# Sparse attention's compression in pairs of positions and two steps; all gates of tile 1 of layer 0 beside the first tile's experts

## The reference

```
for each of 2 layers:
  (queries, keys, values, gate logits m_g ...) = split(x @ w_in)
  o_a .. o_d = stick-breaking, sparse (NSA), retention, gated linear attention   # 4 x 256 wide
  proj  = each o @ its w_branch                              # 256 -> 1024
  gates = sigmoid(m_g)                                       # positions x 4 x 1024
  x = layer_norm(al * x + (sum of gates * proj) @ w_out)
  x = layer_norm(al * x + peer_ffn(x))                       # 8 heads x 16 experts per position
```

## Time and profile before

| | us |
|---|---|
| median of 3 runs | 2868.34 |
| lowest, highest | 2865.76, 2875.42 |
| the profiled execution | 2872.7 |
| its span, first to last instruction | 2870.9 |
| PE busy | 2357.6 (82%) |
| DVE busy | 1347.6 (47%) |
| ACT busy | 1304.0 (45%) |
| POOL busy | 749.1 (26%) |
| mean granted TensorE clock, of 2.4 GHz | 0.882 |
| HBM read | 836.06 MB |

### The profile page before, as it was taken

The page is one execution under the profiler, slowest core; times in us unless marked ns, Lnnn a source line. Parts: engine busy times, 40 slices in busy tenths (PEclk is TensorE's granted clock), DMA queues, the critical chain, the costliest instruction groups (busy, mean ns, idle before and its releaser), DMA issues.

```text
span 2870.9 us, 34220 instructions
## 1 busy us (share of the span) xinstructions
PE 2357.6 (82%) x13592; PEld 2004.4 (70%) x13592; DVE 1347.6 (47%) x3159; ACT 1304.0 (45%) x2330; POOL 749.1 (26%) x614
## 2 busy tenths in 40 slices
PE   7989998999999999878676878686788787666676
PEld 6878887877866878767555867566687675565554
DVE  3652333421002323665556764545765544686444
ACT  2741113100000311476746576754567764556665
POOL 0021112200000000333344323333323333434664
PEclk9989999999999999996687998899798999776666
DMA  6221211233435568998799999999998999999997
GB/s 247 105 88 62 85 52 45 81 132 126 162 151 200 197 249 346 402 418 326 283 415 415 411 421 376 392 420 416 391 421 351 420 368 416 404 376 355 421 421 324
DMA packets 110000, 839.35 MB, mean 292 GB/s; under 512 B 12176, under 2 KB 12432, under 8 KB 13968
## 3 DMA queue, kind: packets, MB, share of 16 engines
q0 software_dynamic: 73728, 536.90, 46.3%
q1 hardware_dynamic: 36112, 300.25, 26.6%
HBM read 836.06 MB, written 1.05 MB: 292 GB/s over the span
## 4 chain that ended last, share of the span: by engine, by line
PE 52%; DMA 21%; DVE 11%; ACT 10%; issue 4%; POOL 1%; SPq 0%; POOLq 0%; DVEq 0%; ACTq 0%
DMA mem<-in_puv,mem 20%; PE psm L443 11%; PE psm L2246 7%; PE psm L1816 5%; PE psm L451 5%; DVE mem L2290 4%; PE psm L756 4%; ACT mem L2264 4%; PE psm L2121 3%; PE psm L1351 3%; PE psm L1454 2%; PE psm L2008 2%; ACT L2259 1%; PE psm L1502 1%; PE psm L447 1%
## 5 line engine op out<-in xcount | busy, mean ns | idle before, releaser
L2246 PE MATMUL psm<-mem 128*128 128x128 f32 x4096 | 696.0, 327 | 370.9 <-ACT mem L2264 370.2
L2246 PEld LDWEIGHTS psm<-mem 128*128 128x128 f32 x4096 | 579.2, 170 | 483.7 <-ACT mem L2264 465.2
L2274 POOL DMA_INDIRECT mem<-in_puv,mem x512 | 627.7, 1226 | 1100.4 <-PE psm L2246 1022.4
L2290 DVE CUSTOM_DVE_ANT_0 mem<-mem 128x1024 f32<-128x1024 f32 x512 | 624.8, 1225 | 431.7 <-DMA mem<-in_puv,mem 431.2
L2264 ACT ACTIVATE mem<-mem 128x1024 f32<-128x1024 f32 x512 | 588.8, 1150 | 16.7
L443 PE MATMUL psm<-mem 128*128 128x256 f32 (+2 forms) x1376 | 313.1, 390 | 3.1 <-DVE mem L1291 1.5
L2259 ACT ACTIVATE mem<-mem 128x1 f32<-128x1 f32 x512 | 101.8, 199 | 454.9 <-DVE mem L2290 454.1
L443 PEld LDWEIGHTS psm<-mem 128*128 128x128 f32 x1376 | 261.8, 192 | 53.3 <-issue 14.8
L1816 PE MATMUL psm<-mem 128*128 128x256 f32 x1024 | 245.0, 392 | 0.7 <-ACT mem L1530 0.5
L451 PEld LDWEIGHTS psm<-mem 128*128 128x128 f32 x1440 | 187.0, 195 | 48.8 <-issue 21.9
L451 PE MATMUL psm<-mem 128*128 128x128 f32 x1440 | 199.1, 283 | 23.3 <-DVE mem L1126 6.8
(11 more groups left out here) (364 smaller groups left out, 2414.5 us busy)
## 6 DMA issues: line engine op xcount, KB each, us to landing
mem<-in_w2g SPq DMA_DIRECT2D x64, 1024.0 KB, 8.3
mem<-in_w SPq DMA_DIRECT2D x18, 2048.0 KB, 7.7
mem<-in_pwq SPq DMA_DIRECT2D x32, 1024.0 KB, 11.9
mem<-in_w2f SPq DMA_DIRECT2D x28, 1024.0 KB, 10.5
mem<-in_wgu SPq DMA_DIRECT2D x11, 2048.0 KB, 7.7
mem<-in_w2t SPq DMA_DIRECT2D x20, 1024.0 KB, 11.8
mem<-in_w2b SPq DMA_DIRECT2D x16, 1024.0 KB, 10.6
mem<-in_w2o SPq DMA_DIRECT2D x16, 1024.0 KB, 9.7
```

Source lines behind the costliest of these rows:

```text
L2246: m = pe.matmul(bank(6 + c // 4)[:, tsl(c % 4)], GR[n % PING][:, 1024 + c * 128:1152 + c * 128], ident, is_transpose=True, start=k == 0 an ...
L2274: po.indirect_dma_start(GR[n % PING], None, A[f"puv{i // 2}"], bass.IndirectOffsetOnAxis(ap=IX[i % 2][:, k:k + 1], axis=0)).then_inc(gsem[ ...
L2290: ve.tensor_tensor_reduce(out=GR[n % PING][:, 0:1024], in0=GR[n % PING][:, 0:1024], in1=X[:, i % 2, :], scale=1.0, scalar=0.0, op0=MUL, op ...
```

## The change

The compression takes two positions at a time. `GP_` becomes [key or value][16 pairs][blocks], with the even position's 64 channels in partitions 0 to 63 and the odd one's in 64 to 127; the weights are laid out so outside the kernel. TensorE has 16 matmuls for keys and 16 for values, over 128 partitions, and a `yield` between them puts the two in two plan steps. VectorE writes `GP_` with eight adds instead of two. `nsa` has 23 steps instead of 22, and the streams on ScalarE and VectorE get one empty step more. The exception for tile 1's gates goes: they are woven into its attention in stage 1 as for the other tiles, with banks 0 and 1, and the last 36 steps of tile 0 are mix, query and route alone.

```
--- before.py
+++ after.py
@@ -259,12 +259,11 @@
 
         def tile_steps(i):
             front = ["fm"] * 28 + ["ht1"] * (i == 0) + ["tm"] * 4 + weave([("tm", 10, 1), ("core", 7, 0.7)])
-            attend = weave([("gates", 32 * (i != 1), 1), ("nsa", 22, 1), ("core", 14, 0.7)])
+            attend = weave([("gates", 32, 1), ("nsa", 23, 1), ("core", 14, 0.7)])
             return front + attend + ["mix"] * 24 + ["query"] * 8 + ["route"] * 20
 
         plan = [(s, 0) for s in tile_steps(0)[:-36]]
-        plan += [(s, int(s == "gates")) for s in weave([("mix", 8, 0.5), ("gates", 12, 1)]) + ["query"] * 8
-                 + weave([("route", 20, 1), ("gates", 20, 1)])]
+        plan += [(s, 0) for s in tile_steps(0)[-36:]]
         for i in RI:
             placed_at = [(128.0 * i + k, ("e", 128 * i + k)) for k in range(128)]
             placed_at += [(128.0 * i + 1.1 + 0.1 * k, ("fin", i - 1)) for k in range(4) if i >= 1]
@@ -286,7 +285,7 @@
         used = {}
         uses = dict(fm=[("f", n, 4 * n, min(4 * (n | 1) + 3, 27)) for n in range(7)],
                     tm=[("t", 0, 0, 3)] + [("t", n, 2 * n + 2, (7, 7, 11, 11, 13)[n - 1]) for n in range(1, 6)],
-                    nsa=[("cw", 0, 0, 1)], gates=[("g", n, 2 * n, 4 * (n // 2) + 3) for n in range(16)],
+                    nsa=[("cw", 0, 0, 2)], gates=[("g", n, 2 * n, 4 * (n // 2) + 3) for n in range(16)],
                     mix=[("b", n, 2 * n + 2, 2 * n + 3) for n in R4] + [("o", n, 12 + n, 12 + (n | 1)) for n in R4] + [("ga", 0, 19, 21)],
                     query=[("q", n, 4 * n, 8 * (n // 2) + 7) for n in R8], fin=[("gf", 0, 8, 9)])
         step, nth2, last2 = {}, {}, {}
@@ -1552,8 +1551,6 @@
             if i == 0:
                 pe.wait_ge(*KV[1, 0])
                 pe.wait_ge(*KA[1, 4])
-            if i == 1:
-                pe.wait_ge(*GTA[1, 7])
             pe.matmul(bank(4)[:, 0:128], walpha, LR[0:16, :], start=True, stop=True).then_inc(YP.next((i, "al")), 1)
             yield
             yield
@@ -1798,15 +1795,11 @@
 
 
         def gates_bank(i, j):
-            return bank(4 * (i == 1) + j % 2)
+            return bank(j % 2)
 
         def gates_pe(pe, i):
             t = i % 2
-            if i == 1:
-                pe.wait_ge(*BA_[0, ("m", 0)])
-                pe.wait_ge(*BV[0, ("m", 1)])
-            else:
-                pe.wait_ge(*MA[i, ("t", 5)])
+            pe.wait_ge(*MA[i, ("t", 5)])
             for n in range(16):
                 W = slot2(("g", i, n), 8, 256)
                 pe.wait_ge(*landed2("g", i, n))
@@ -1831,7 +1824,7 @@
 
 
         KS, KW = at(scr, 256), at(scr + 256, 256)
-        GP_ = at(scr + 512, 32, 15)
+        GP_ = at(scr + 512, 2, 16, 15)
         KC, VC = at(scr + 1024, 16), at(scr + 1040, 64)
         PS, PCm, PT = at(scr + 1104, 2, 256), at(scr + 1616, 16), at(scr + 1632, 5, 128)
         NG = SM[:, 24:36]
@@ -1852,14 +1845,15 @@
         def nsa_pe(pe, i):
             t = i % 2
             nb, ns = 7 + 8 * t, 128 * (t + 1)
-            CW = slot2(("cw", i, 0), 32, 64)
+            CW = slot2(("cw", i, 0), 2, 16, 64)
             yield
             pe.wait_ge(*landed2("cw", i, 0))
             pe.wait_ge(*XV[i, "gp"])
-            for k in range(32):
-                pe.matmul(bank(2)[0:64, 0:nb], CW[0:64, k, :], GP_[0:64, k, 0:nb], start=k == 0, stop=k == 31)
-            for k in range(32):
-                m = pe.matmul(bank(3)[0:nb, 64:128], GP_[64:128, k, 0:nb], CW[64:128, k, :], start=k == 0, stop=k == 31)
+            for k in range(16):
+                pe.matmul(bank(2)[0:64, 0:nb], CW[:, 0, k, :], GP_[:, 0, k, 0:nb], start=k == 0, stop=k == 15)
+            yield
+            for k in range(16):
+                m = pe.matmul(bank(3)[0:nb, 64:128], GP_[:, 1, k, 0:nb], CW[:, 1, k, :], start=k == 0, stop=k == 15)
             m.then_inc(XP.next((i, "kc")), 1)
             yield
             for h in R4:
@@ -1920,9 +1915,14 @@
                 for pb in (0, 64):
                     ve.tensor_copy(dst[pb:pb + 64, 0:ns], FK[p0:p0 + 64, 2, 0:ns])
             kv3 = FK[:, 3, :].rearrange("p (c i) -> p i c", i=16)
-            for hf in R2:
-                e = ve.tensor_tensor(GP_[:, 16 * hf:16 * hf + 16, 0:nb], kv3[:, :, hf:hf + nb], bc(posT[:, 16 * hf:16 * hf + 16], 2, nb), ADD)
+            for kv in R2:
+                p = slice(64 * kv, 64 * kv + 64)
+                for par in R2:
+                    for hf in R2:
+                        e = ve.tensor_tensor(GP_[64 * par:64 * par + 64, kv, 8 * hf:8 * hf + 8, 0:nb], kv3[p, par::2, hf:hf + nb],
+                                             bc(posT[p, 16 * hf + par:16 * hf + 16:2], 2, nb), ADD)
             e.then_inc(XV.next((i, "gp")), 1)
+            yield
             yield
             ve.wait_ge(*XP[i, "kc"])
             ve.tensor_copy(KC[0:64, 0:nb], bank(2)[0:64, 0:nb])
@@ -2609,9 +2609,9 @@
         b = I["w_branch_2"][L].reshape(2, 2, 2, 128, 2, 512)
         acc["w2b"].append(b.transpose(4, 0, 3, 1, 2, 5).reshape(4, 128, 2048))
         acc["w2o"].append(chunks(I["w_out_2"][L], 256))
-        ck = [I[n][L].reshape(32, 64, 64).transpose(1, 0, 2).reshape(64, 2048)
+        ck = [I[n][L].reshape(16, 128, 64).transpose(1, 0, 2).reshape(128, 1024)
               for n in ("nsa_cmp_wk_2", "nsa_cmp_wv_2")]
-        acc["cmpw"].append(cat(ck, 0))
+        acc["cmpw"].append(cat(ck, 1))
         wa = np.zeros((128, 128), w.dtype)
         wa[0:16] = I["gla_w_alpha_2"][L]
         pos = I["nsa_cmp_pos_2"][L].T
```

## The result

| | before | after |
|---|---|---|
| median (runs), us | 2871.73 (4) | 2819.95 (4) |
| ratio to the kernel before | | 0.9822, 95% interval 0.9801 to 0.9843 |
| profiled execution, its span, us | 2872.7, 2870.9 | 2820.1, 2818.2 |

The change takes 51 us off by the ratio (51.8 between the medians, 52.7 between the spans). Cut at the same events, the two profiled executions differ so; the last column is what the prediction's steps gave.

A forecast was written before the change was run, and what follows sets the result against it. TensorE bounds the head before the first expert, DMA transfers mostly the expert stages, with idle DMA time in stage 1. Next tile's first dot product -16, stages 2 and 3 5 each: -26 from 2868.3, forecast 2841 us, range 2818 to 2860.

The forecast's parts named there:

- (a): Tile 0's layer norm: twelve gate steps leave, transposes come 14 us earlier, less 4 for a slow clock; net 10 us.
- (b): Tile 0's route: twenty gate steps leave, first dot product 7 instead of 13 us after the first fetch; 6 us.
- (d): Stage 1: all 32 gate steps of tile 1 move in, 40 us of DMA time; stage forecast at 458 us.
- (c): Compression, four tiles: half the matmul records in two steps; 7 us on tile 0, 5 in each of stages 2 and 3.
- rival C: More given back: clock kept in the norm, compression worth 8 a stage, stage 1 shorter; -41, 2827 us; chance 0.13.
- The attention's later steps all come one plan step later: Attention after the compression: its steps move one plan step back, with compression weights loaded in the same size; put at 0.
- the two shorter steps with a transpose between: Compression in the stages: should give back about half the lost DMA time, 5 us each in stages 2 and 3.
- Rival B: Stage 1: gates paid in full at the DMA engines, 40 us added; -9, 2859 us; chance 0.22 with its twin.
- rival D: Stage 1's front: gate loads and expert rows share DMA queues, early start lost; 491 us, total 2885; chance 0.05.
- B's twin: Compression saves nothing: -26 + 17 = -9, the same result as Rival B; chance 0.22 together with it.

The follow-up runs named there:

- e1: Kernel before with the new compression alone, tile 1's gates left beside tile 0's mix and route: 2830.3 us, ratio 0.9860 to the kernel before.
- e4: Changed kernel with the old 64-row compression matmuls, keys and values in two plan steps: ratio 0.9867 to the kernel before.
- e8: Changed kernel with the old 64-row compression in one step and an empty step after it: 2853.9 us, ratio 0.9937 to the kernel before.
- e2: Changed kernel with the old compression (64 rows, one step), so the gates' move alone: 2869.2 us, ratio 0.9994 to the kernel before.
- e5: Changed kernel with the new 128-row compression in one step and an empty step after it: ratio 0.9826 to the kernel before.
- e3: Changed kernel with the new 128-row compression in one step, no second step anywhere: 2836.8 us, ratio 0.9883 to the kernel before.
- e6: Changed kernel with 2 of 8 matmuls in each chain of tile 1's layer 0 gates, all loads kept: ratio 0.9821 to the kernel before.
- e7: Changed kernel loading one eighth of each of tile 1's layer 0 gate weights, all matmuls kept: 2813 us, ratio 0.9785 to the kernel before.

## Why the prediction was right, and where its sizes were wrong

The time, 2820 us, lies in the range at its fast end, which was 2818; the forecast was 26 us less than before and 51 came. The direction and the mechanisms of (a), (b) and (d) were right. That the time still fell within the range is partly luck: (c) and (d) were both too cautious, and the fast end had been set by rival C "with some more in (c)". Two of the prediction's own signs lay just outside as well: stage 1 at 446.4 us where 450 to 465 was given, and pieces of 1.95 to 2.04 us where 2 to 3.5 was.

(a) and (b), the head: right in mechanism and size. Norm's row, transposes, exponential and TensorE's late start all went as worked out; -18.6 us measured over the three stretches against -16. The clock did fall in the idle time, at 2.6 us for the 4 that were put.

(c), the compression: right in sign, and the term that was mis-sized. The prediction gave it 7 + 5 + 5 and took 5 off stage 1: 22 us. e1 measured 40. The 7 before the first expert came (7.5 in e1, from the first gate matmul on); the 5 a stage did not: e1's stages 1 to 3 were 11.0, 9.3 and 13.7 us shorter. Two things were missed. The half was too little: the prediction counted records, and took the values' 95 to 109 ns a record for a cost per instruction, though the keys' 61 ns stood beside it; at one clock they cost the same (e4: 3.74 and 3.90 us), and the run itself had lowered the clock. And "The attention's later steps all come one plan step later", with "I put 0", is the term that failed: e8 against e2 and e5 against e3 put it at 16 us. The prediction looked for what the added step costs and not for what it moves. That the cut helps ("the two shorter steps with a transpose between") is right for the long run only; with 128 rows e5 shows nothing in it.
The Trainium skill (TensorE: Matmul & The Clock Gate, LDWEIGHTS) says that rows don't count in a weight load. The rows of after agree: a 128-row record takes 2.03/32 = 63 ns, a 64-row one 61, and the median weight load of the keys' 64 columns 138 ns with 128 rows and 135 with 64.

(d), the gates in stage 1: the mechanism was right, they fill idle DMA time; the size was off by half. Stage 1 was forecast at 458, taken from stage 3, and came at 446.4. The forecast had the move add 12 us (451 less 5 for the compression, to 458); compared with e1 it adds 6, for 16.8 MB. Rival B (40 us added) and rival D are refuted by that. B's twin, a compression that saves nothing, is refuted by e1. Rival C comes nearest in the number, and by (c), for which it had 8 us a stage, not by the clock: the clock was not kept in (a), and in stage 1 it went to 0.88, while e6 with a clock of 0.85 is as fast.
The Trainium skill (DMA: Bandwidth & Descriptors, SWDGE vs HWDGE vs iDMA) has the DMA engines take turns between the two queues. No run singles that out; if it slowed the fetches in stage 1, it did so within the 6 us.

The move alone was worth nothing measurable (e2). The prediction's own sum for it, 16 us in the head against 12 in stage 1, gives 4 us, which agrees, though e2 had 20 and 16. What it didn't say is that the two parts depend on each other. By the ratios the move brings 0.0006, 2 us, without the new compression and 0.0038, 11 us, with it. The two are only just told apart by these numbers; the 16 and 6 us that it costs stage 1 point the same way.

## What to carry to other kernels

Count a run of small matmuls not by its instructions alone: look at whether the clock falls within it and stays low behind it, and what the engines that it delays were feeding. When several streams are dealt into one order, an added step moves everything behind it; test that apart, with an empty step, before the gain is put down to what the step does. To move loads into a stage costs at least what its idle DMA time doesn't cover, so read length x (1 - rate / full rate) first: with the new compression 35 us were idle, 40 were moved in, and 6 were paid. It can cost more: with the old compression 45 were idle and 16 were paid all the same (e2). And taking loads out again can give as little back (e7: 35 us of transfers, 7 us).

## What the runs showed of the hardware

Sixty-four small records with 64 moving columns took 3.74 us behind other work (e4) and 5.96 to 7.0 us directly behind 64 others (e8 and the kernel before). In e8 TensorE was busy for 6.00 of 6 us and then 8.00 of 8, and the granted clock was 0.59 and 0.50 in them: it fell to the 1.2 GHz level all the same. That an engine is busy by the profile isn't enough to hold the clock.
